# A two-block transformer kernel: two adaption vectors summed on GpSimd, and silu built from tanh

## What is computed

```python
c_act = jax.nn.silu(c)
for layer in range(DEPTH):
    ada = jnp.einsum('bd,de->be', c_act, w_ada[layer]) + b_ada[layer]
    shift, scale, gate = jnp.split(ada, 3, axis=-1)
    h = rms_norm(x, norm_g[layer]) * (1.0 + scale[:, None, :]) + shift[:, None, :]
    y = even_mixer(h, ...) if layer % 2 == 0 else odd_mixer(h, ...)
    x = x + gate[:, None, :] * y
```

## Time and profile before

| what | value |
|---|---|
| median of 3 runs | 1543.26 us (1541.81 to 1543.28) |
| profiled execution, its own time | 1541.57 us |
| its span, first to last instruction | 1539.7 us |
| PE busy / DVE busy / ACT busy / POOL busy | 1519.3 / 1026.7 / 440.1 / 12.4 us |
| even layer's attention steps (0 to 18) | about 1235 to 1358 us of the span |

### The profile page before, as it was taken

How to read it: one execution, slowest core, us unless ns; L and a number is a source line. 1 busy time by engine, 2 the same in 40 slices (tenths; PEclk the granted TensorE clock), 3 DMA queues, 4 the chain that set the end, 5 groups by cost and what they waited for, 6 DMA issues and landing times.

```text
span 1539.7 us, 27734 instructions
## 1 busy us (share of the span) xinstructions
PE 1519.3 (99%) x11151; PEld 1348.8 (88%) x11151; DVE 1026.7 (67%) x1928; ACT 440.1 (29%) x932; POOL 12.4 (1%) x26
## 2 busy tenths in 40 slices
PE   8999999999999999999999999999999999999998
PEld 7998869898899999899878899799999787678887
DVE  5788886477667774678897467667775564545562
ACT  5415424012100001335423211300011456524431
POOL 1000000000000000100000000000000000000000
PEclk9999999999999999999999999999999999999999
DMA  8543453353475444344242442475454745553320
GB/s 271 190 165 111 150 153 111 112 204 123 143 241 164 153 171 175 120 164 152 100 162 87 163 149 91 145 274 165 158 178 158 255 152 219 219 195 118 133 103 28
DMA packets 172385, 243.40 MB, mean 158 GB/s; under 512 B 16830, under 2 KB 95332, under 8 KB 172260
## 3 DMA queue, kind: packets, MB, share of 16 engines
q1 hardware_dynamic: 170372, 237.96, 45.0%
q10 hardware_dynamic: 1888, 3.67, 0.7%
HBM read 240.56 MB, written 1.05 MB: 157 GB/s over the span
## 4 chain that ended last, share of the span: by engine, by line
PE 95%; DVE 2%; ACT 1%; issue 1%; DMA 0%; SPq 0%; DVEq 0%; POOL 0%; ACTq 0%
PE psum L629 34%; PE psum L1644 27%; PE psum L1499 6%; PE psum L1299 3%; PE psum L3108 3%; PE psum L445 2%; PE psum L1558 2%; PE psum L1294 2%; PE psum L3200 2%; PE psum L428 2%; PE psum L1428 1%; PE psum L461 1%; PE psum L3208 1%; PE psum L663 1%; PE psum L1400 1%; PE psum L1339 1%
## 5 line engine op out<-in xcount | busy, mean ns | idle before, releaser
L629 PE MATMUL psum<-hT,ring 128*128 128x256 f32 x1552 | 342.8, 380 | 0.4 <-ACT hT L3305 0.2
L629 PEld LDWEIGHTS psum<-hT,ring 128*128 128x128 f32 x1552 | 292.8, 190 | 44.4 <-issue 6.4
L629 PE MATMUL psum<-uT,ring 128*128 128x256 f32 x384 | 84.9, 380 | 0.0
L1644 PE MATMUL psum<-hT,ring 128*128 128x128 f32 x704 | 82.3, 275 | 1.0 <-issue 1.0
L629 PEld LDWEIGHTS psum<-uT,ring 128*128 128x128 f32 x384 | 72.8, 190 | 10.2 <-DVE uT L1162 0.6
L1644 PEld LDWEIGHTS psum<-hT,ring 128*128 128x128 f32 x704 | 80.4, 192 | 1.4 <-issue 1.4
L1925 ACT ACTIVATE SCR<-SCR 128x512 f32<-128x512 f32 x22 | 13.9, 630 | 219.9 <-DVEq L2709 219.9
L510 DVE TENSOR_TENSOR psum<-psum,const 128x512 f32<-128x512 f32 (+4 forms) x41 | 22.1, 559 | 65.5 <-PE psum L445 64.5
L491 ACT ACTIVATE SCR<-psum,stats 128x128 f32<-128x128 f32 (+2 forms) x128 | 49.7, 405 | 23.0 <-DVE stats L524 22.9
L1644 PE MATMUL psum<-G,ring 128*128 128x128 f32 x400 | 47.8, 276 | 0.0
L1920 ACT ACTIVATE SCR<-psum 128x256 f32<-128x256 f32 (+1 forms) x30 | 10.7, 355 | 127.9 <-PE psum L1644 127.9
(11 more groups left out here) (647 smaller groups left out, 3008.5 us busy)
## 6 DMA issues: line engine op xcount, KB each, us to landing
ring<-in_w_in SPq DMA_DIRECT2D x46, 1024.0 KB, 7.0
ring<-in_ffn_w_gate_up SPq DMA_DIRECT2D x88, 512.0 KB, 5.7
ring<-in_w_ada SPq DMA_DIRECT2D x24, 1024.0 KB, 7.9
ring<-in_ffn_w_down SPq DMA_DIRECT2D x16, 1024.0 KB, 6.1
ring<-in_w_in_odd SPq DMA_DIRECT2D x16, 1024.0 KB, 7.4
ring<-in_w_in_even SPq DMA_DIRECT2D x10, 1024.0 KB, 7.0
ring<-in_x_w_kv SPq DMA_DIRECT2D x8, 1024.0 KB, 5.9
ring<-in_ssm_w_glu SPq DMA_DIRECT2D x8, 1024.0 KB, 6.3
```

What stands on the lines that cost most here:

```text
L629: ins = nc.tensor.matmul(b[0:width, n * S:n * S + S], w[k // 4][:, k % 4, c0[n]:c0[n] + width], tile(k), start=k == 0, stop=k == kt - 1)
L1644: ins = nc.tensor.matmul(banks[job][:, at:at + P], left, right, start=first, stop=last)
```

## The change

Two things are done. First, ada11 and ada12 leave PE: GpSimd multiplies each of the eight weight slices (128x512) by the matching column of silu(c) and adds them up, 15 instructions a part, each waiting for the one before. PE still transposes the sum, and DVE now adds 128 columns instead of 4. Their four weight pieces move forward in the ring (ada11 to behind qb, ada12 to behind w1k, both ahead of zb), their slots are free again only when GpSimd has read them, and the fillers of steps 8 to 18 are dealt out anew. Second, silu(z) is made as 0.5 z (1 + tanh(z/2)): ACT writes the tanh to a tile of its own, DVE makes z (1 + tanh) in one instruction per group, and the factor 0.5 goes into the multiplication by the attention output.

```diff
-    def dve(self, nc, dve, link, i):
+    def dve(self, nc, dve, link, i, before_store=None):
...
+        if before_store:
+            before_store()
         if 0 <= i - PAIR_LAG - 1 < len(self.u):
             self.stored(nc, dve, i - PAIR_LAG - 1)
...
-    def ada_turned(layer, n):
+    def ada_turned(layer, n, summed=None):
         b = ojobs.begin(pe, f"ada{layer}{n} turned")
-        jobs.evacuated(pe, f"ada{layer}{n}")
+        if summed:
+            pe.wait_ge(*summed)
+        else:
+            jobs.evacuated(pe, f"ada{layer}{n}")
...
-def ada_store(V, dve, link, m, ojobs, layer, n):
+def ada_store(V, dve, link, m, ojobs, layer, n, rows=4):
...
-    b = ojobs.full(dve, name).rearrange("p (i s k) -> p i s k", i=4, s=4)
+    b = ojobs.full(dve, name).rearrange("p (i s k) -> p i s k", i=4, s=rows)
...
-           7: ["zb3", "silu b"], 8: ["za0"], 9: ["za1"], 10: ["za2"], 11: ["za3", "silu a"], 12: ["ada11"], 13: ["ada12"],
-           14: ["ada13"], 15: ["part ada11"], 16: ["part 0"], 17: ["part 1"],
-           18: ["part ada12", "part 2", "part ada13"]}
...
+           7: ["zb3", "tanh b"], 8: ["za0"], 9: ["za1"], 11: ["za2"], 12: ["za3", "tanh a"], 13: ["ada13"], 16: ["part 0", "part ada11"], 17: ["part 1"],
+           18: ["part 2", "part ada12", "part ada13"]}
...
+ADA_POOL = [1, 2]
-SECOND_O += ["b heads0", "b heads1", "b heads2", "ada11 turned", "b heads3", "ada12 turned", "ada13 turned", "square 2"]
+SECOND_O += ["b heads0", "b heads1", "b heads2", "b heads3", "ada11 turned", "ada12 turned", "ada13 turned", "square 2"]
...
     def ada(layer, n):
-        wide(f"ada{layer}{n}", a["w_ada_2"], 512 * n, 512, f"ada{layer}{n}", layer)
+        last = "vw" if layer == 1 and n in ADA_POOL else f"ada{layer}{n}"
+        wide(f"ada{layer}{n}", a["w_ada_2"], 512 * n, 512, last, layer)
...
+    ada(1, 1)
...
     for x in "vk":
         for n in range(2):
             piece(f"w1{x}.{n}", a[f"cmp_w1_{x}_2"], 8 * n, 8, 0, CMP_H, f"hidden {x}")
+    ada(1, 2)
     wide("zb", w, E_ZB, 512, "zb3")
     wide("za", w, E_ZA, 512, "za3")
-    for n in (1, 2, 3):
-        ada(1, n)
+    ada(1, 3)
...
+    tanhs = {x: at.rearrange("p (k t) -> p k t", t=S) for x, at in (
+        ("b", m["hg"]), ("a", m["vm"][:, :, :].rearrange("p t n -> p (t n)")), ("c", G[:, 4096:5120]), ("d", G[:, 5120:6144]))}
...
     def stored(c0, c):
-        return lambda nc_, b: nc_.vector.tensor_tensor(z[:, c0 + c, :], b[:, 0:S], z[:, c0 + c, :], ALU.mult)
+        return lambda nc_, b: nc_.vector.scalar_tensor_tensor(
+            out=z[:, c0 + c, :], in0=b[:, 0:S], scalar=0.5, in1=z[:, c0 + c, :], op0=ALU.mult, op1=ALU.mult)
...
                 elif name.startswith("part ada"):
-                    ada_turned(1, int(name[9]))
+                    n = int(name[9])
+                    ada_turned(1, n, (sig["ada_summed"], 15 * ADA_POOL.index(n) + 15) if n in ADA_POOL else None)
...
-        def silu(x):
-            at, names = SILU[x]
+        def tanh(x):
+            at, names = GATES[x]
             if isinstance(names, str):
                 act.wait_ge(sig["seven_made"], SEVENS.index(names) + 1)
             else:
                 for name in names:
                     jobs.evacuated(act, name)
-            nc.scalar.activation(z[:, at:at + 4, :], z[:, at:at + 4, :], ACT.Silu).then_inc(sig["silu"], 1)
+            nc.scalar.activation(tanhs[x], z[:, at:at + 4, :], ACT.Tanh, scale=0.5).then_inc(sig["tanh"], 1)
...
-                    ada_copy(1, n, {1: None, 2: None, 3: "04"}[n])
+                    ada_copy(1, n, "04")
...
+    @block.gpsimd
+    def _(pool):
+        link = Chain(pool, (sig["ada_summed"], [0]))
+        c, part = m["c_wide"][:, :, 0], m["vx"][:, 0, :]
+        pool.wait_ge(sems["named"][0]["c_spread"], 1)
+        jobs.full(pool, "vw")
+        for n in ADA_POOL:
+            total = m["ada_rows"][(6 + n) % ADA_SLOTS]
+            for h in range(2):
+                w = ring.arrived(pool, f"ada1{n}.{h}")
+                for k in range(4):
+                    by = c[:, 4 * h + k:4 * h + k + 1]
+                    if h == k == 0:
+                        link(nc.gpsimd.tensor_scalar(total, w[:, k, :], by, None, ALU.mult))
+                    else:
+                        link(nc.gpsimd.tensor_scalar(part, w[:, k, :], by, None, ALU.mult))
+                        link(nc.gpsimd.tensor_tensor(total, total, part, ALU.add))
...
-        def gated(dst, src, silus, *stores):
+        def twice_silu(x):
+            dve.wait_ge(sig["tanh"], "bacd".index(x) + 1)
+            at = z[:, GATES[x][0]:GATES[x][0] + 4, :]
+            link(V.scalar_tensor_tensor(out=at, in0=tanhs[x], scalar=1.0, in1=at, op0=ALU.add, op1=ALU.mult))
+
+        def gated(dst, src, *stores):
             for name in stores:
                 ojobs.evacuated(dve, name)
-            dve.wait_ge(sig["silu"], silus)
-            V.tensor_tensor(dst, dst, src, ALU.mult).then_inc(sig["gated"], 1)
+            V.scalar_tensor_tensor(out=dst, in0=src, scalar=0.5, in1=dst, op0=ALU.mult,
+                                   op1=ALU.mult).then_inc(sig["gated"], 1)
...
-            if i == 6 + PAIR_LAG + 1:
-                dve.wait_ge(sig["silu"], 1)
             att_ab.dve(nc, dve, link, i)
+            if i == 8:
+                twice_silu("b")
...
-                gated(z[:, 0:4, :], a_out, 2, *(f"a heads{c}" for c in range(4)))
+                twice_silu("a")
+                gated(z[:, 0:4, :], a_out, *(f"a heads{c}" for c in range(4)))
             if i == 16:
-                ada_store(V, dve, link, m, ojobs, 1, 1)
+                ada_store(V, dve, link, m, ojobs, 1, 1, P)
             if i == 18:
-                ada_store(V, dve, link, m, ojobs, 1, 2)
+                ada_store(V, dve, link, m, ojobs, 1, 2, P)
                 ada_store(V, dve, link, m, ojobs, 1, 3)
                 gains(1)
...
-            if i == 1 + PAIR_LAG + 1:
-                dve.wait_ge(sig["silu"], 3)
-            if i == 6 + PAIR_LAG + 1:
-                dve.wait_ge(sig["silu"], 4)
-            att_c.dve(nc, dve, link, i)
+            att_c.dve(nc, dve, link, i, (lambda: twice_silu("c")) if i == 1 + PAIR_LAG + 1 else None)
...
-                gated(z[:, 4:6, :], c_out[:, 4:6, :], 4, "c heads4", "c heads5")
+                twice_silu("d")
+                gated(z[:, 4:6, :], c_out[:, 4:6, :], "c heads4", "c heads5")
...
+        summed |= {f"{DEPTH} ada1{n}.{h}": (sems["named"][DEPTH]["ada_summed"], 15 * i + 8 * h + 7)
+                   for i, n in enumerate(ADA_POOL) for h in range(2)}
```

More of the change, by code:

```diff
@@ L576, in pair_jobs @@
             names += [f"{u} turned {s}" for s in range(1 if u.endswith("cmp") else 2)]
-        names += [x for x in (fill or {}).get(i, []) if not x.startswith(("silu", "part"))]
+        names += [x for x in (fill or {}).get(i, []) if not x.startswith(("tanh", "part"))]
     return names
@@ L947, in first_block_layer @@
     o_done = shared["o_done"]
-    dve_step, act_step, pool_step = (shared[n] for n in ("dve_step", "act_step", "pool_step"))
+    dve_step, act_step = (shared[n] for n in ("dve_step", "act_step"))
     negmax_ready, rows_ready = shared["negmax_ready"], shared["rows_ready"]
@@ L2778 @@
            4: ["zb0", "hidden v turned", "hidden k turned"], 5: ["zb1", "k cmp", "v cmp"], 6: ["zb2"],
[3 rows of a table removed]
-C_FILL = {0: ["q1", "k1"], 1: ["Z0 a", "Z0 b"], 2: ["q2", "k2"], 3: ["Z0 c", "Z0 d", "silu c"], 4: ["q3", "k3"],
-          5: ["V1 a", "V1 b"], 6: ["V1 c", "V1 d", "Z1 a"], 7: ["Z1 b", "Z1 c", "Z1 d", "silu d"],
+           7: ["zb3", "tanh b"], 8: ["za0"], 9: ["za1"], 11: ["za2"], 12: ["za3", "tanh a"], 13: ["ada13"], 16: ["part 0", "part ada11"], 17: ["part 1"],
+           18: ["part 2", "part ada12", "part ada13"]}
+C_FILL = {0: ["q1", "k1"], 1: ["Z0 a", "Z0 b"], 2: ["q2", "k2"], 3: ["Z0 c", "Z0 d", "tanh c"], 4: ["q3", "k3"],
+          5: ["V1 a", "V1 b"], 6: ["V1 c", "V1 d", "Z1 a"], 7: ["Z1 b", "Z1 c", "Z1 d", "tanh d"],
           8: ["part 0", "part 1"], 9: ["part 2"]}
@@ L2789 @@
 TURNS = ["qa0", "qa1", "ka", "kw", "kvc", "qb0", "qb1"] + [f"{x}{n}" for n in range(4) for x in "qk"]
-SILU = {"a": (0, ["za0", "za1", "za2", "za3"]), "b": (4, ["zb0", "zb1", "zb2", "zb3"]), "c": (0, "Z0"), "d": (4, "Z1")}
+GATES = {"a": (0, ["za0", "za1", "za2", "za3"]), "b": (4, ["zb0", "zb1", "zb2", "zb3"]), "c": (0, "Z0"), "d": (4, "Z1")}
+ADA_POOL = [1, 2]
 ADA_FIRST = [(0, 4), (0, 5), (1, 0)]
 SECOND_O = [f"ada{l}{n} turned" for l, n in ADA_FIRST] + [f"a heads{c}" for c in range(4)]
-SECOND_O += ["b heads0", "b heads1", "b heads2", "ada11 turned", "b heads3", "ada12 turned", "ada13 turned", "square 2"]
+SECOND_O += ["b heads0", "b heads1", "b heads2", "b heads3", "ada11 turned", "ada12 turned", "ada13 turned", "square 2"]
 SECOND_O += [f"ada1{n} turned" for n in (4, 5)] + [f"c heads{c}" for c in range(8)] + ["square 3"]
@@ L3125, in ab_fill @@
                 n = int(name[-1]) if name[-1].isdigit() else None
```

(17 more changed lines are left out.)

## The result

The changed kernel takes 1553.74 us (median of 6 runs, 1553.01 to 1554.62) where the kernel before takes 1542.69 beside it: ratio 1.0076, 95% interval 1.0066 to 1.0086, so 11.05 us slower. The forecast was 1553, range 1546.5 to 1558. The profiled execution has a span of 1551.5 us, 11.8 more than before.

A forecast was written before the change was run, and what follows sets the result against it. PE's fixed order, busy 1519.3 of 1539.7 us, was taken as the bound. 7.1 + 2.5 + 2.3 - 1.9 = +10.0 on 1541.57 gives 1551.6; the median stands 1.69 above, so 1553, range 1546.5 to 1558.

The forecast's parts named there:

- Part 1: Before zb0 on PE: zb's weights, issued behind qb1 and ada12, land late; a new wait of 7.1 us (6.7 to 7.4).
- Part 2: zb0, right behind that new wait: PE's work runs slower after the pause, 2.5 us lost (ends: nothing and 2.5).
- Part 3: Before unit 0's transposes: GpSimd's sum of ada11 holds up DVE, 2.3 us of waiting (0 to 5).
- Rival (a): zb0: the clock holds through the wait, so 2.5 less, 1551 us; chance 0.13.
- Rival (b): Unit 0's transposes: DVE locked out for whole GpSimd instructions, a 5 us wait, steps 5 and 6 slower; 1557 us; chance 0.14.
- Part 4: Steps 8 to 18: 6.0 us removed, 4.1 us of new waits added, net -1.9 us (-3.4 to -0.4).
- (c): zb0: zb pieces not late, and steps without fillers close up; -3.7 us, 1539.6, faster; chance 0.06.
- (d): Whole kernel: it cancels; 7.1 us wait, no clock loss or contention, full 6.0 back; 1544.4 us; chance 0.07.
- (e): ACT's tanh: it loads tables after all, 0.6 us more, 1553.9 us; chance 0.05.

## Why the prediction was right

**Part 1 (7.1) was right in kind and place**, and measured 7.8. zb.1 landed 13.5 us behind qb1's end where I had 13.0, and zb0 began 0.2 behind that. The run with the earlier ring order, which has neither the wait nor the slow zb0, shows the cause.

**Part 2 (2.5) was right in kind and size**: 1.6 in the changed kernel's profile, and in the four experiments with the same wait zb0 took 5.70, 6.19, 6.38 and 6.52, so the cost is 1.6 to 2.9 from one execution to another. The size came from the pause at the start, where the clock does not read as fallen, so that it fits is in part luck. Rival (a) is out: the granted clock, 1.00 around the pause at the start and so no evidence, reads 0.55 here.

**Part 3 (2.3) had the right place**, step 2, and measured 1.4. What I took for a partial share of every access is a full block by additions and a smaller one by products. Rival (b) had the size of a block right and its reach wrong; I had no row of a GpSimd addition.

**Part 4 (-1.9) is the step that failed**: it measured +1.0. Its waits were right (4.1 forecast, 4.1 measured, each at its place), and so was what was removed. The term that was missing is the clock: I had costed it behind the one long wait, and read the tail's waits as time alone. With steps 14 and 15 emptied the granted clock went to 1.2 GHz for some 7 us, which cost 2.9; with those steps filled it stayed at 2.4 GHz. That the total came out all the same is luck: the missing 2.9 more than makes up for what parts 2 and 3 measured less: +0.7 - 0.9 - 0.9 + 2.9 is 1.8, the 11.8 less the 10.0 forecast.

**Rivals (c), (d) and (e)** are out: zb was late, nothing cancelled, tanh loads no table. I had said that waits of much more than 4 us in part 4 would show the forecast wrong; they did not come, and the loss was in slower work, which a view of waits does not show.

## What to carry to other kernels

Putting weights for an idle engine ahead in an in-order ring delays everything behind them: read from the queue's time line which job the next piece will then wait for. Where a step loses its filler, cost the waits and also the clock behind them: here 4.1 us of short waits were followed by 2.9 of slower matmuls, which no view of waits names. Work taken from a full engine need not gain its whole length: a job of 1.9 us, summed on GpSimd, was worth 0.6 to 1.2, and the new order of the same work, without GpSimd, gave about as much (1.2 under the kernel before). That it was DVE which set the pace is inferred from its 3.9 busy us of every 4 in one run, not shown by one that relieves it.

## What was unexpected of the hardware

GpSimd's product by a column takes longer than its addition of two tensors. Groups of instructions on POOL, changed kernel:

```profile
L3453 POOL TENSOR_SCALAR vx<-ring,c_wide 128x512 f32<-128x512 f32 x14 | 22.6, 1612 | 1.4
L3454 POOL TENSOR_TENSOR cT<-cT,vx 128x512 f32<-128x512 f32 x7 | 8.9, 1267 | 0.6
```

1.61 us with one SBUF tensor and a column, 1.27 with two tensors; and it is the shorter one that holds up DVE more. The other surprise is that the clock fell in the tail without a pause longer than 1.9 us, and once, in the run that filled only that pause, while PE was at work again (granted clock 1.00 to 1343.5, 0.73 in the half microsecond behind it), with one wait of 0.68 ahead of it.
